# Two 64-row products of a bias laid on the two row halves of TensorE's array, and retention's products with the state issued for two heads side by side

## The reference, cut to what matters

```python
h = rms_norm(x, norm1_g); proj = h @ w_in                    # 1024 x 3072
# retention, in four chunks of 128 tokens, q and k 64 wide, v 128 wide, per head
y = (q_i k_i^T * decay) @ v_i  +  (q_i * q_decay) @ state_{i-1}
state_i = chunk_decay * state_{i-1} + (k_i * k_decay)^T @ v_i
x = x + concat(diff_attention, silu(g) * rms_norm(y)) @ w_o
# experts: for each block of 128 rows x_b of expert e
u = x_b @ w_in[e] + b_in[e]                                  # 1024 x 2048, b_in is 2048 wide
act = min(glu, 7) * sigmoid(1.702 * glu) * (clip(lin, -7, 7) + 1)
y_b = act @ w_out[e] + b_out[e]                              # 1024 x 1024
out = rms_norm(x + sum over a token's four experts)
```

## Time and profile before

| | before |
|---|---|
| median of three runs | 1472.73 us |
| the profiled execution | 1473.39 us |
| its span in the trace | 1471.7 us |
| mean granted TensorE clock | 0.998 |
| PE, PEld, DVE, ACT busy | 98%, 80%, 87%, 69% |
| HBM traffic over the span | 340 GB/s |

### The profile page before, as it was taken

How to read it: one execution, slowest core, us unless ns; L and a number is a source line. 1 busy time by engine, 2 the same in 40 slices (tenths; PEclk the granted TensorE clock), 3 DMA queues, 4 the chain that set the end, 5 groups by cost and what they waited for, 6 DMA issues and landing times.

```text
span 1471.7 us, 21956 instructions
## 1 busy us (share of the span) xinstructions
PE 1441.0 (98%) x6833; PEld 1183.4 (80%) x6833; DVE 1277.7 (87%) x1120; ACT 1019.0 (69%) x876; POOL 240.9 (16%) x232
## 2 busy tenths in 40 slices
PE   7999899999999999999999999999999999999997
PEld 6888578778888888888888888888888888888885
DVE  5465747799999999999999999999999999999998
ACT  5423734667777777777777777777777777777774
POOL 0100302412111111111111111212111111111111
PEclk9999999999999999999999999999999999999999
DMA  9442101899999999999999999999999999999994
GB/s 342 177 182 120 44 0 66 303 345 373 365 371 357 375 363 370 367 364 379 364 376 371 379 368 358 389 369 363 373 372 368 370 367 372 367 375 365 367 358 168
DMA packets 131391, 471.72 MB, mean 321 GB/s; under 512 B 15304, under 2 KB 15596, under 8 KB 131176
## 3 DMA queue, kind: packets, MB, share of 16 engines
q1 hardware_dynamic: 118160, 451.46, 81.7%
q0 software_dynamic: 13024, 19.88, 5.5%
q10 hardware_dynamic: 184, 0.08, 0.0%
HBM read 467.44 MB, written 32.51 MB: 340 GB/s over the span
## 4 chain that ended last, share of the span: by engine, by line
PE 91%; DVE 4%; issue 2%; ACT 2%; DMA 1%; DVEq 0%; ACTq 0%
PE pair L993 24%; PE pair L985 24%; PE pair L987 24%; PE pair L714 3%; PE pair L719 3%; PE pair L715 3%; PE pair L999 2%; PE pair L1011 2%; PE pair L975 2%; DVE split L1815 1%; PE pair L856 1%; PE pair L871 1%; PE pair L858 1%; DMA ring<-in_w_moe_in 1%; ACT split L1325 0%
## 5 line engine op out<-in xcount | busy, mean ns | idle before, releaser
L1815 DVE TENSOR_TENSOR split<-ring,split 128x2048 fp32r<-128x2048 f32 x396 | 891.8, 2288 | 71.4 <-ACT split L1325 71.2
L1325 ACT CAST split<-ring 128x2048 fp32r<-128x2048 f32 x396 | 760.0, 1920 | 193.1 <-PE pair L993 190.7
L985 PE MATMUL pair<-split,operands 128*128 128x512 f32 x1584 | 630.0, 398 | 1.0 <-DVE operands L1821 1.0
L987 PE MATMUL pair<-split,operands 128*128 128x512 f32 x1584 | 618.0, 390 | 0.0
L993 PE MATMUL pair<-split,operands 128*128 128x512 f32 x1584 | 424.8, 390 | 0.9 <-DVE split L1815 0.9
L993 PEld LDWEIGHTS pair<-split,operands 128*128 128x128 f32 x1584 | 297.1, 188 | 65.1 <-DVE split L1815 2.1
L985 PEld LDWEIGHTS pair<-split,operands 128*128 128x128 f32 x1584 | 297.7, 188 | 60.1 <-DVE operands L1821 1.4
L987 PEld LDWEIGHTS pair<-split,operands 128*128 128x128 f32 x1584 | 297.9, 188 | 58.5
L2094 POOL DMA_INDIRECT expert_sums<-work,list_cur x32 | 61.8, 1932 | 455.3 <-PE pair L993 423.8
L2087 POOL DMA_INDIRECT work<-h_rows,token_next x34 | 75.2, 2211 | 183.4 <-DMA token_next<-slot_lists 166.7
L1334 ACT CAST operands<-pair 128x512 fp32r<-128x512 f32 x66 | 38.8, 589 | 68.8 <-PE pair L993 39.9
(11 more groups left out here) (268 smaller groups left out, 1149.4 us busy)
## 6 DMA issues: line engine op xcount, KB each, us to landing
ring<-in_w_moe_in SPq DMA_DIRECT2D x264, 1024.0 KB, 9.1
ring<-in_w_moe_out SPq DMA_DIRECT2D x132, 1024.0 KB, 9.9
ring<-in_w_in SPq DMA_DIRECT2D x12, 1024.0 KB, 10.5
ring<-in_w_o SPq DMA_DIRECT2D x4, 1024.0 KB, 10.3
resid<-in_x SPq DMA_DIRECT2D x4, 512.0 KB, 5.2
expert_sums<-zero_rows SPq DMA_DIRECT2D x4, 512.0 KB, 11.9
h_rows<-work SPq DMA_DIRECT2D x4, 512.0 KB
work<-expert_sums SPq DMA_DIRECT2D x4, 512.0 KB, 5.2
```

The source lines that it names most:

```text
L985: pe.matmul(dst[:, f, :], left_hi[:, k0 + k, :], hi[c.buffer][:, k, cols], start=(start and k == 0), stop=False)
L987: pe.matmul(dst[:, f, :], left_lo[:, k0 + k, :], hi[c.buffer][:, k, cols], start=False, stop=False)
L1325: act.copy(hi[c.buffer], raw[c.slot]).then_inc(hi_made, 1)
L1815: dve.tensor_tensor(lo[c.buffer], raw[c.slot], hi[c.buffer].bitcast(F32), ALU.subtract).then_inc(lo_made, 1)
```

## The change

`bias_of_half` takes for bank f only the 64 rows that hold its biases: rows 0 to 63 of both operands for bank 0, rows 64 to 127 for bank 1. The number of products and their columns stay. In `ret_output` the loop runs over pairs of heads: first the two products with the state (heads 2q and 2q+1, on the two row halves, into two banks), then the two products of 128 rows.

```diff
@@ ret_output(i)
-                for h in range(NH):
-                    rows = slice(64 * (h % 2), 64 * (h % 2) + 64)
-                    dst = pair[ret_out_at[i]][:, h % 2, (h // 2) * P:(h // 2 + 1) * P]
+                for q in range(NH // 2):
+                    dst = [pair[ret_out_at[i]][:, r, q * P:(q + 1) * P] for r in range(2)]
                     if i >= 1:
-                        pe.matmul(dst, qdT[rows, h // 2, i * P:(i + 1) * P], state[rows, i - 1, h // 2, :],
-                                  start=True, stop=False)
-                    mm = pe.matmul(dst, st_s[:, i, h % 2, h // 2, :],
-                                   proj[:, i, CRV + h * P:CRV + (h + 1) * P], start=(i == 0), stop=True)
+                        for r in range(2):
+                            rows = slice(64 * r, 64 * r + 64)
+                            pe.matmul(dst[r], qdT[rows, q, i * P:(i + 1) * P], state[rows, i - 1, q, :],
+                                      start=True, stop=False)
+                    for r in range(2):
+                        h = 2 * q + r
+                        mm = pe.matmul(dst[r], st_s[:, i, r, q, :],
+                                       proj[:, i, CRV + h * P:CRV + (h + 1) * P], start=(i == 0), stop=True)
@@ bias_of_half(g)
                 for f in range(2):
-                    pe.matmul(pair[g][:, f, :], pick_bias[:, f, :], b_in_parts[:, g * 512:(g + 1) * 512],
+                    rows = slice(f * 2 * NE, (f + 1) * 2 * NE)
+                    pe.matmul(pair[g][:, f, :], pick_bias[rows, f, :], b_in_parts[rows, g * 512:(g + 1) * 512],
                               start=True, stop=False)
```

## The result

The changed kernel takes 1486.88 us (median of 8 runs, 1484.57 to 1488.55) beside 1476.96 us of the kernel before on the same chips (8 runs, 1472.57 to 1481.54). The ratio is 1.0074, 95% interval 1.0055 to 1.0092: slower by 0.7%, some 11 us. The forecast was 1482.8 us against 1472.73 us, ratio 1.0069. The kernel before has a higher median here (8 runs instead of the 3 that the forecast started from), so the ratio and not the time itself is what compares with the forecast. The profiled execution took 1487.14 us, 13.75 us more than that of before.

What follows compares the result with a forecast made beforehand. PE was taken to bound the expert stage; bias pairs at +11.7 us and retention at -1.6 us gave +10.1 us on 1472.73 us, so 1482.8 us, range 1476 to 1491 us.

Steps and rivals of the forecast that it cites:

- Bound: Expert stage: PE, busy 200.00 of 200 us, sets the pace, so a nanosecond on PE is one on the kernel.
- Way in: Ahead of a bias pair: the first 64-row product starts 0.32 us after the last 128-row one, not 0.227.
- The pair: Bias pair: the two 64-row products run side by side, the second starting 0.01 us after the first.
- Uncovered load and way out: Bias pair to next product: 0.10 us for weights not loaded ahead, 0.32 us until a 128-row product may begin.
- Restart: Behind the bias pair: the first 128-row product's weights load uncovered, so its step takes 0.34 us.
- Retention: Products with the state: each of three calls 1.21 us shorter, of which 0.2, 1.2 and 0.2 arrive, -1.6 us.
- Sum: Whole kernel: +11.7 us from 65 bias pairs at 0.18 and -1.6 us from retention, together +10.1 us.
- A: Bias pairs: crossings hidden by PE's queue, a pair costs one step; -15.9 us, 1456.8 us; chance 7%.
- B: Bias pairs: fp32r products on 64 rows run serially; +25 us, 1497.8 us; chance 7%.
- C: Expert stage: loads, not PE, set the pace, so PE's loss falls into idle time; 1471.1 us; chance 6%.

Runs made afterwards that it cites:

- half_and_whole: The kernel before with only the bias edit, and only the first product of each pair cut to 64 rows, the second on 128; ratio 1.0163, pass 36.28 us.
- one_half: The kernel before with only the bias edit, but both products of a pair on rows 0 to 63; ratio 1.0170, pass 36.33 us.
- pair_twice: The kernel before with only the bias edit, each 64-row pair issued twice; ratio 1.0191, pass 36.36 us.
- ret_gate: The kernel before with only the retention edit, and DVE gating chunk 2 before evicting chunk 1's transposes; ratio 0.9989, pass 35.48 us.
- no_bias: The kernel before without the bias products of the inner layer; ratio 0.9810, pass 34.57 us.
- before_look2: The kernel before, unchanged, run again for another trace of the first pass; no ratio given.

## Why the prediction was right

- **Bound.** That PE alone sets the pace of a pass held in both directions: +0.41, +0.80, +0.85, +0.88 and -0.91 us a pass all appeared in the pass, with PE at 200.00 of 200.
- **Way in.** 0.32 us forecast from the score products behind the projection, 0.318 measured. The type of the products is the same on both sides here, so the delay goes with the row count; that the 128-row product has to leave the array first is how I read it. The Trainium skill, TensorEngine Tiling (Array Packing), section Key Properties, says that changing the tiling mode drains TensorE. The trace agrees and adds the price: half_and_whole has 0.20 us a crossing with the load.
- **The pair.** 0.01 us apart was forecast, 0.003 to 0.004 measured; one_half shows that the overlap is worth 0.22 us. The prediction took the 0.70 us of the earlier trace rows for two whole products; they are the first records of the two, one on each half. Its conclusion stands, since the two start together.
- **Uncovered load and way out.** 0.10 + 0.32 forecast, 0.43 measured from the pair to the next product, and pair_twice shows the parts: 0.33 - 0.227 = 0.10 and 0.32.
- **Restart.** 0.34 forecast from the earlier trace rows, 0.34 measured. The term stopped there, and that is what it missed: the next five products or so take 0.23 to 0.24 us each where a running stream takes 0.227, so a pair costs 0.204 us over a pass instead of 0.18. 65 x 0.024 = 1.6 us more. The kernel before shows this too behind the place of the earlier trace rows, where "0.23" was read as the running step: from 250.943 to 251.871 four steps take 0.232 each. Its cause is open. In half_and_whole the product behind the way out is a bias product, and there the steps are 0.33 and then 0.227 at once.
- **Retention.** Forecast 0.2, 1.2 and 0.2 us of 1.21 each. Measured 1.37 us up to `mix_high(0)` and 1.61 up to `mix_high(1)`, with the two waits at L835 and L859 where they were forecast. ret_gate takes away the second and gets 0.97 us of the remaining 1.0. That the gain is carried holds up to the expert stage; in the first pass it can be lost again, which the prediction didn't foresee.
- **Sum.** 65 x 0.204 - 1.6 = +11.7 us by the terms as measured, +10.1 forecast, about +11 by the ratio, whose interval is +8 to +14 us. So the time bears out the direction and the rough size; it is the trace that bears out the terms. That the forecast lies within 1 us of the ratio is in part luck, as the missed 1.6 us show.
- **Rivals.** A (crossings hidden) is refuted by the changed kernel's own rows, B (halves in turn) by one_half, C (loads set the pace) by no_bias.

## What to carry to other kernels

Two products over half of the rows save a step only if they don't stand alone: look at what is ahead of and behind them. In a stream of full-height products each way into and out of the half-height kind costs nearly a step of 512 columns here (0.20 against 0.227 us), so a single pair loses, and even a second pair in the same place only breaks even (pair_twice: 0.44 us above before, where two more full-height products would take 0.45). Where the kinds alternate already, as in retention, grouping them saves crossings (3.16 us of the second call became 1.95), and what remains to be checked is which wait comes last once PE is early.

## What the runs showed of the hardware that was not expected

A pause of 2.99 us on PE is followed in some executions of the same kernel by products at half clock and in others not: up to 8 products at 0.43 us instead of 0.23. The later passes repeat to 0.01 us, so in the traces most of the scatter comes from the first pass, which took from 36.0 to 43.9 us in 14 traces, and from what stands ahead of it: in before_look2 the granted clock was at 0.50 from 198.5 to 208.5 us, and the second `mix_high` came 27.06 us after the first product with the state instead of 22.51. And a start with uncovered weights can leave a trace: behind it several products run at 0.23 to 0.24 us, in kernels with and without the edit, though not in half_and_whole.
